# A hybrid mLSTM and attention layer on one core: cache places, weight splits and head squares moved between two attention stages

## What is computed

```
def diff_weights(scores, lam):
    p = jax.nn.softmax(scores, axis=-1)
    return p[:, :, 0] - lam * p[:, :, 1]

# prompt: blocks of 128 queries against the keys up to their chunk
s = jnp.einsum('bqhcd,bkhcd->bhcqk', qb, k) * scale      # two scores per head (c)
o = jnp.einsum('bhqk,bkhd->bqhd', diff_weights(s, lam), vf)
# sample: 16 queries of each of 8 batches against 256 cached and 16 new keys
k_all = jnp.concatenate([cache_k, dk], axis=1)
v_all = jnp.concatenate([cache_v, dv], axis=1)
# both: a norm of each head (mean of squares over 128), gains, then the projection
y_m = mlstm_readout(hm, o_gate, g)        # rms_norm(h, g) * o_gate
y_d = diff_readout(o, g, lam_init)        # rms_norm(o, g) * (1 - lam_init)
out = jnp.concatenate([y_m, y_d], axis=-1) @ w_out
```

## Time and profile before

| what | value |
|---|---|
| median of three runs | 1366.63 us (1360.15 to 1367.04) |
| the profiled execution | 1368.47 us, its span 1366.7 us |
| PE busy | 1296.9 us, 95% |
| DVE, ACT, POOL busy | 59%, 43%, 24% |
| granted clock of PE, mean | 0.966 of full |

### The profile page before, as it was taken

One profiled execution on the slowest core, in us unless ns is written; L12 is line 12 of the kernel. 1 busy time (PEld: TensorE's weight loads), 2 busy tenths in 40 slices (PEclk: granted clock), 3 DMA queues, 4 the chain that ended last, 5 costly groups with the idle time before them and its releaser, 6 DMA issues.

```text
span 1366.7 us, 23094 instructions
## 1 busy us (share of the span) xinstructions
PE 1296.9 (95%) x8072; PEld 1139.9 (83%) x8072; DVE 800.7 (59%) x1420; ACT 583.7 (43%) x1146; POOL 322.1 (24%) x276
## 2 busy tenths in 40 slices
PE   4999999999999997999999788979999999999997
PEld 3899999999878886888877455868999999988886
DVE  3767667767433755252427854258676667654484
ACT  5533434434333645422213565337344444433463
POOL 0633434343100000001010604007444443410000
PEclk9999999999999998999998698989999999999999
DMA  9655454454555741322230235131322232134563
GB/s 316 188 154 153 153 153 153 144 160 127 199 201 180 237 158 38 123 87 68 91 108 13 74 105 175 31 108 47 108 77 87 82 92 80 43 123 153 196 220 138
DMA packets 167152, 175.84 MB, mean 129 GB/s; under 512 B 10377, under 2 KB 139921, under 8 KB 167098
## 3 DMA queue, kind: packets, MB, share of 16 engines
q1 hardware_dynamic: 165754, 171.31, 39.0%
q0 software_dynamic: 1344, 3.81, 0.9%
HBM read 165.79 MB, written 9.05 MB: 128 GB/s over the span
## 4 chain that ended last, share of the span: by engine, by line
PE 90%; ACT 4%; DVE 3%; issue 2%; DMA 1%; SPq 0%; DVEq 0%; ACTq 0%
PE ps L1243 86%; DMA resid<-in_x_sample 1%; PE ps L1285 1%; PE ps L1818 1%; DVE y L2136 0%; ACT x_norm L769 0%; ACT modulated_pairs L820 0%; PE ps L1511 0%; ACT w_sums_hi L833 0%; PE ps L1564 0%; ACT h_sums_hi L843 0%; DMA k_cache<-in_cache_k 0%; PE ps L1778 0%; DVE w_lo L1934 0%; PE ps L1905 0%
## 5 line engine op out<-in xcount | busy, mean ns | idle before, releaser
L1243 PE MATMUL ps<-h_sums_hi,w_sums_hi 128*128 128x320 f32 x1216 | 376.3, 314 | 3.0 <-ACT h_sums_hi L799 2.0
L1243 PE MATMUL ps<-h_sums_hi,w_sums_lo 128*128 128x320 f32 x1216 | 371.0, 309 | 0.0
L1243 PE MATMUL ps<-h_sums_lo,w_sums_hi 128*128 128x320 f32 x1216 | 370.9, 309 | 0.0
L1934 DVE TENSOR_TENSOR w_lo<-w_raw,w_hi 128x1024 fp32r<-128x1024 f32 (+2 forms) x106 | 147.2, 1389 | 201.2 <-ACT w_hi L920 125.8
L1243 PEld LDWEIGHTS ps<-h_sums_hi,w_sums_hi 128*128 128x128 f32 x1216 | 227.4, 188 | 14.1 <-issue 10.0
L1243 PEld LDWEIGHTS ps<-h_sums_hi,w_sums_lo 128*128 128x128 f32 x1216 | 227.5, 188 | 0.0
L1243 PEld LDWEIGHTS ps<-h_sums_lo,w_sums_hi 128*128 128x128 f32 x1216 | 227.5, 188 | 0.0
L861 ACT ACTIVATE silu_gate<-silu_gate 128x320 f32<-128x320 f32 x80 | 37.9, 474 | 283.8 <-DVE silu_gate L2038 283.8
L920 ACT ACTIVATE w_hi<-w_raw 128x1024 fp32r<-128x1024 f32 x88 | 93.3, 1061 | 139.1 <-PE ps L1243 111.5
L1934 DVE TENSOR_TENSOR w_sums_lo<-w_raw,w_sums_hi 128x512 fp32r<-128x512 f32 x132 | 113.7, 865 | 44.0 <-ACT w_sums_hi L857 43.6
L1243 PE MATMUL ps<-w_hi,h_t_hi 128*128 128x512 f32 (+2 forms) x360 | 135.5, 376 | 2.8 <-DVE h_t_lo L1934 1.7
(11 more groups left out here) (333 smaller groups left out, 1832.3 us busy)
## 6 DMA issues: line engine op xcount, KB each, us to landing
w_raw<-in_w_ffn_out SPq DMA_DIRECT2D x88, 512.0 KB, 4.1
w_raw<-in_w_ffn_in SPq DMA_DIRECT2D x86, 512.0 KB, 3.8
w_raw<-in_w_ada SPq DMA_DIRECT2D x28, 1024.0 KB, 5.0
w_raw<-in_w_in SPq DMA_DIRECT2D x10, 1024.0 KB, 5.1
w_raw_start<-in_w_ada SPq DMA_DIRECT2D x8, 1024.0 KB, 8.4
w_raw<-in_w_out SPq DMA_DIRECT2D x4, 1024.0 KB, 6.4
k_cache<-in_cache_k SPq DMA_DIRECT2D x8, 512.0 KB, 5.0
v_cache<-in_cache_v SPq DMA_DIRECT2D x8, 512.0 KB, 4.1
```

Of the source, the lines that this page charges most:

```text
L1243: return pe.matmul(out, lhsT, rhs, start=start, stop=stop)
L1934: return dve.tensor_tensor(dst, raw, hi.bitcast(F32), ALU.subtract)
```

## The change

The cache has three places; batch b uses place b % 3, and nothing of it lies in `w_raw` any longer. The sync queue does not wait for group 7's splits before the caches; it waits for `st_out`, fills places 0 and 1, waits for `m_hn` and fills place 2. Then the keys of batch b wait for the transposes of batch b - 3, and the values for the output of batch b - 3, with one key load ahead of the values of the batch before. The wait for group 7's splits now stands in front of the second half of the output weights. DVE's two splits of group 7 move from steps 4 and 6 of the prompt attention to the ends of batches 2 and 4 of the sample's. The five sets of mLSTM head squares move from steps 0 to 4 to steps 6 to 10. The diff, without the lines that only replace an index by b % 3:

```diff
-        CACHE = (0, 1, 2, 3, 0, 1, 2, 0)
-
-        def cache_sems(b):
-            s = CACHE[b]
-            return (kc_landed[s], vc_landed[s]) if s < 3 else (e_landed[0], e_landed[1])
...
                 elif g == 8:
                     mixer_loads()
-                    for s in range(2):
-                        sp.wait_ge(g_hi[s], g)
-                        sp.wait_ge(g_lo[s], g)
                     continue
...
             sp.wait_ge(st_out, 16 * 11)
-            sp.wait_ge(m_hn, 2 * NT)
-            for b in range(4):
+            for b in range(3):
+                if b == 2:
+                    sp.wait_ge(m_hn, 2 * NT)
                 keys_load(b)
                 values_load(b)
-            for b in range(4, DB):
-                used = (0, 1, 2, 4)[b - 4]
-                sp.wait_ge(s_ktr, 2 * (used + 1))
-                keys_load(b)
-                sp.wait_ge(s_o, used + 1)
-                values_load(b)
-
-            sp.wait_ge(s_ktr, 2 * 4)
-            sp.wait_ge(s_o, 4)
+            for b in range(3, DB + 1):
+                if b < DB:
+                    sp.wait_ge(s_ktr, 2 * (b - 2))
+                    keys_load(b)
+                if 3 < b <= DB:
+                    sp.wait_ge(s_o, b - 3)
+                    values_load(b - 1)
+
             for s in range(2):
+                sp.wait_ge(g_hi[s], 8)
+                sp.wait_ge(g_lo[s], 8)
                 sp.dma_start(grp_view(RAW, s, 512), w_o[:, 4 * s:4 * s + 4, 512:1024]).then_inc(g_landed[s], 16)
...
-                if n < NT:
+                if 6 <= n < 6 + NT:
                     act.wait_ge(m_head, 2 * NT)
-                    head_squares(0, n, HHM[:, n, :])
+                    head_squares(0, n - 6, HHM[:, n - 6, :])
...
                 p_combine(n)
-                if n in (4, 6):
-                    grp_lo(7, (n - 4) // 2)
...
                 if b == 1:
                     dve.wait_ge(gate_bc, 2)
                     gate(1)
+                elif b in (2, 4):
+                    grp_lo(7, b // 2 - 1)
```

More of the change, by code:

```diff
@@ L243, in build @@
         C3 = 108 * KB + 264 * NT * 4 + 10 * KB
-        KC = [at("k_cache0", A0, [P, 2, 512]), at("k_cache1", A0 + 4 * KB, [P, 2, 512]), at("k_cache2", C3, [P, 2, 512]),
-              at("k_cache3", 60 * KB, [P, 2, 512])]; A0 += 8 * KB
-        VC = [at("v_cache0", A0, [P, 2, 512]), at("v_cache1", A0 + 4 * KB, [P, 2, 512]), at("v_cache2", C3 + 4 * KB, [P, 2, 512]),
-              at("v_cache3", 64 * KB, [P, 2, 512])]; A0 += 8 * KB
+        KC = [at("k_cache0", A0, [P, 2, 512]), at("k_cache1", A0 + 4 * KB, [P, 2, 512]), at("k_cache2", C3, [P, 2, 512])]; A0 += 8 * KB
+        VC = [at("v_cache0", A0, [P, 2, 512]), at("v_cache1", A0 + 4 * KB, [P, 2, 512]), at("v_cache2", C3 + 4 * KB, [P, 2, 512])]; A0 += 8 * KB
         KCT = [at("k_cache_t0", A0, [P, HD, PAST]), at("k_cache_t1", 20 * KB, [P, HD, PAST])]; A0 += 4 * KB
         QBD = at("q_blocks", A0, [P, DB, HD, 32]); A0 += 4 * KB
-        VN = [at("v_new0", A0, [DS, 512]), at("v_new1", A0 + 2 * KB, [DS, 512]), at("v_new2", 110 * KB, [DS, 512]), at("v_new3", 68 * KB, [DS, 512])]; A0 += 4 * KB
+        VN = [at("v_new0", A0, [DS, 512]), at("v_new1", A0 + 2 * KB, [DS, 512]), at("v_new2", 110 * KB, [DS, 512])]; A0 += 4 * KB
         assert A0 <= 60 * KB
@@ L525, in grp_view @@
             return T[:, s, 0:4 * n].rearrange("p (k n) -> p k n", k=4)
-        CACHE = (0, 1, 2, 3, 0, 1, 2, 0)
-        def cache_sems(b):
-            s = CACHE[b]
-            return (kc_landed[s], vc_landed[s]) if s < 3 else (e_landed[0], e_landed[1])
-        def cache_landed(b, values):
-            n = 16 * ADA_FIRST if CACHE[b] == 3 else 0
-            return cache_sems(b)[values], n + (32 if values else 16) * CACHE[:b + 1].count(CACHE[b])
         def sample_heads(T, k):
@@ L708, in _ @@
                         sp.dma_start(v, w[:, 4 * s:4 * s + 4, c0:c0 + n]).then_inc(g_landed[s], 16)
+            sp.wait_ge(st_out, 16 * 11)
             def keys_load(b):
[L711 removed]
+                sp.dma_start(KC[b % 3][:, :, :], k_cache[:, b, :, :]).then_inc(kc_landed[b % 3], 16)
             def values_load(b):
[L714 to L719 removed]
+                sp.dma_start(VC[b % 3][:, :, :], v_cache[:, b, :, :]).then_inc(vc_landed[b % 3], 16)
+                sp.dma_start(VN[b % 3][:, :], DVT[b * DS:(b + 1) * DS, NTP, :]).then_inc(vc_landed[b % 3], 16)
+            for b in range(3):
+                if b == 2:
+                    sp.wait_ge(m_hn, 2 * NT)
                 keys_load(b)
                 values_load(b)
[L722 to L730 removed]
+            for b in range(3, DB + 1):
[5 more added lines that the diff above has]
+                    values_load(b - 1)
             for s in range(2):
+                sp.wait_ge(g_hi[s], 8)
+                sp.wait_ge(g_lo[s], 8)
                 sp.dma_start(grp_view(RAW, s, 512), w_o[:, 4 * s:4 * s + 4, 512:1024]).then_inc(g_landed[s], 16)
@@ L1810, in s_key_transposes @@
             def s_key_transposes(b):
-                pe.wait_ge(*cache_landed(b, 0))
+                pe.wait_ge(kc_landed[b % 3], 16 * (b // 3 + 1))
                 if b >= 2:
@@ L1817, in s_key_transposes @@
                     for h in range(HD):
-                        q = pe.transpose(PS[:, 6 * (b % 2) + k, h * P:(h + 1) * P], KC[CACHE[b]][:, k, h * P:(h + 1) * P], ident)
+                        q = pe.transpose(PS[:, 6 * (b % 2) + k, h * P:(h + 1) * P], KC[b % 3][:, k, h * P:(h + 1) * P], ident)
                     q.then_inc(s_ktr, 1)
@@ L1844, in s_out @@
                 pe.wait_ge(s_pt, 2 * (b + 1))
-                pe.wait_ge(*cache_landed(b, 1))
+                pe.wait_ge(vc_landed[b % 3], 32 * (b // 3 + 1))
                 if b:
@@ L1851, in s_out @@
                         probs = PTS[:, k, rows] if k < 2 else PTS[0:DS, k, rows]
-                        values = VC[CACHE[b]][:, k, cols] if k < 2 else VN[CACHE[b]][:, cols]
+                        values = VC[b % 3][:, k, cols] if k < 2 else VN[b % 3][:, cols]
                         q = mm(PS[rows, 5, 0:DV], probs, values, k == 0, k == 2)
```

4 lines of the change are left out of this document (removed).

## The result

The changed kernel took 1357.77 us (median of 5 executions, 1356.97 to 1361.75) beside 1366.63 of the kernel before in the same comparison, 1360.15 to 1368.93: a ratio of 0.9947, 95% interval 0.9923 to 0.9971. With 12 further executions its mean is 1359.3 +- 1.2 us; that of the kernel before, from 102 executions beside the experiments, is 1365.5 +- 0.5. All +- in this text are 1.96 standard errors. For a true 95% they are a tenth too narrow with 12 executions and a third too narrow with five or six. So the change brings **6.2 us +- 1.3**; the forecast was 0.9 us slower, at best 5.1 faster than the median. Each execution comes with its mean granted clock of TensorE (PE): 0.9746 in the mean after, 0.9694 before. That turns out to be most of the difference.

The account below looks back on a forecast made before the run. TensorE was taken as the bound, nine tenths of the chain, so only its waits and clock matter: -2.8 prompt attention, +2.0 splits, +1.7 clock, +0.9 us in sum, 1367.5 against the median of 1366.63; range 1361.5 to 1371.5.

Parts of the forecast that it names:

- Early steps of the prompt attention: Before step 8's scores, PE waits removed with the early squares and first split: 1.5 us gained, start at 774.4.
- Steps 8 to 12: Later prompt attention: ACT's queue sets the pace, scores issued in step 12 at 791.6, 2.8 us earlier including the early steps.
- the squares as the sole bound: Steps 6 to 10: with late squares ACT needs 2.8 us a step against PE's 2.25, so ACT sets the pace.
- Loads: Cache loads in both attentions: filling places early is worth nothing, later key loads cost nothing, at worst 0.2 us.
- Splits in the sample's attention: Two splits behind batches 2 and 4 delay exponentials and PE's scores: 2.0 us lost, ends 0.5 and 6.7.
- The prediction's dearer case: Sample's attention: both splits take 3.36 us where POOL is busy throughout, making the sum 1.3 us worse.
- The clock: Sample's attention: new PE pauses of 1.7 and 2.7 us cause one clock fall, 1.7 us lost; ends none and 3.4.
- the clock that holds: Rival, sample's attention: no pause is long enough to cost the clock; -0.8 us, 1365.8; chance 0.22.
- full clock early in the prompt attention: Rival: PE back at 2.4 GHz before 774, gain 4.8, one split covered, no fall; -3.8 us, 1362.8; chance 0.16.
- squares hidden: Rival, prompt attention: ACT has room for the squares, PE goes at its own 2.25 us a step; about 1359.6; chance 0.06.
- The signs: Timeline marks in both attentions: among those for right, step 12's scores near 791.6 and half clock between 824 and 838.

Follow-up runs that it names:

- cache places alone: Kernel before with only the three cache places and the sync queue's new order; squares and splits as before: 1363.95 us, ratio 0.9981.
- early squares without splits: Changed kernel with the five sets of head squares back in steps 0 to 4; splits and caches stay changed: 1359.72 us, ratio 0.9961.
- both splits tiny: Kernel before with both output-weight splits, in steps 4 and 6 of the prompt attention, cut to 16 of 2048 columns: 1359.35 us, ratio 0.9974.
- a quarter of the squares: Changed kernel with one of four heads' squares in each of steps 6 to 10, a constant for the rest: 1358.07 us, ratio 0.9951.
- the splits back: Changed kernel with the two splits back in steps 4 and 6 of the prompt attention; squares and caches stay changed: 1364.22 us, ratio 0.9996.
- tiny splits in the prompt attention: Kernel before with splits there cut to 16 of 2048 columns: both, 1359.35 us; the second alone, 1363.39 us.
- The fillers: Changed kernel with thrown-away matmuls where PE waits anyway: 1357.52 and 1355.88 us in two runs; with 15 more ending the sample's attention, 1355.35 us.
- tiny splits there: Changed kernel with its two splits, in the sample's attention, cut to 16 of 2048 columns: 1360.81 us, ratio 0.9970.
- the squares alone: Kernel before with only the mLSTM head squares moved to steps 6 to 10; splits and cache places as before: 1362.91 us, ratio 0.9990.

## Why the prediction was wrong

It was wrong in the sign of the sum (+0.9 against -6.2), in two terms and by one thing that it left out. Without its clock term the sum is -0.8, and at equal clock the change measures -1.3 +- 0.6: the waits came out near enough in sum, if not one by one. The step that failed is the clock: +1.7 forecast, some -4.9 measured (0.0053 more mean clock at 9.3 us for 0.01).

**Early steps of the prompt attention** (-1.5): right in kind, too small. Where the splits alone differ (cache places alone, and early squares without splits), the stretch from the first scores to step 8's is 19.9 and 19.2 us: 0.7 for the first split, forecast about 0.5. Late squares take it from 19.2 to 17.4, so they free 1.8, forecast about 1.0; I had said that PE's work at half clock nearly fills these steps, but it left 0.34 and 0.67 to 0.81 us in front of two scores. Together 2.5. The other 1.2 of the pair's 3.7 lies between before and the cache places alone, which have the same work here; their clock differs. The granted clock of 760 to 778 was 0.50 before, 0.62 with the cache places alone and 0.72 in the changed kernel.

**Steps 8 to 12** (-1.3): nearly right. From the start of step 8's scores to step 12's I had 17.2 us (791.6 less 774.4); measured are 16.6 (786.15 less 769.53), after 18.5 before. The sum over ACT's queue held, and the waits of 1.05, 0.67 and 1.58 us for ACT show its pace; ahead of the longest ACT also copies the four outputs of a tile. "More than half of what they free goes to the squares" came true as well: the second split's leaving frees 4.6 us, and 2.5 are paid back by the late squares (16.6 against 14.1). What failed is the squares as the sole bound: three quarters of them away freed 1.0, not 2.8.

**Loads** (0): nothing at equal clock, 0.1 +- 0.6. PE's waits for keys were one of 0.42 us, within the sign I gave. In the mean 2.3 +- 2.0 stay unexplained; they go with a clock 0.0023 higher, and I can't say that the cache places cause it.

**Splits in the sample's attention** (+2.0): wrong; they cost 0.2 to 0.3 where batch 5's exponential stands, and nothing in the time. Two inputs failed. I let the second split start at 829.5, where the trace of before has DVE free for it at 828.35, the start of the maximum that would follow it; from there it ends under ACT's two table loads (to 830.83), which were what batch 5's exponential waited for: its row has no wait. I had charged DVE's length to an engine that was busy with its own. And I took 2.7 and 2.7 us for the splits, but they took 2.28. The Trainium skill, GPSIMD Engine Reference, section Specifications, says that POOL's way into SBUF is shared with DVE instructions that have two SBUF inputs. The prediction's dearer case by it, 3.36 us for each split, did not come; here it was POOL that paid. Its product beside the first split took 1.98 us:

```profile
815.25 1.98 POOL L2680 TENSOR_TENSOR diff_heads<-diff_heads,g_diff_rows 128x512 f32<-128x512 f32 x1 [2.29 <-ACT squares L1124]
...
819.64 1.27 POOL L2680 TENSOR_TENSOR diff_heads<-diff_heads,g_diff_rows 128x512 f32<-128x512 f32 x1 [2.41 <-ACT squares L1124]
```

So the trace agrees with the page that the two share something, and not that the split is the one to lose. The kernel before with both splits tiny shows when it does; DVE's rows (the first tiny split, a combination, the second tiny split), then POOL's:

```profile
768.37 0.17 DVE L1934 TENSOR_TENSOR w_lo<-w_raw,w_hi 128x16 fp32r<-128x16 f32 x1
...
772.75 1.37 DVE L2490 SCALAR_TENSOR_TENSOR probs<-probs,max_den 128x256 f32<-128x256 f32 x1
774.04 1.24 DVE L1934 TENSOR_TENSOR w_lo<-w_raw,w_hi 128x16 fp32r<-128x16 f32 x1
```

```profile
772.57 6.53 POOL L2692 TENSOR_TENSOR mlstm_heads<-mlstm_heads,o_gate 128x512 f32<-128x512 f32 x5
```

Sixteen columns took 1.24 us beside POOL, and 0.17 alone: 1.07 more. The whole split took 3.36 beside POOL and 2.28 alone: 1.08 more. The same surplus for 16 and for 2048 columns is not a rate that is shared. It looks as if the split first waited for the product that POOL was in the middle of (1.26 us each), and the reverse where the split had begun first; that is read from the rows, not tested. DVE's combination (1.37 us, and 1.10 the next time, in place of 0.48) is longer beside POOL too, so POOL's five products in a row were a part of what the second split seemed to cost: with both splits tiny PE still stands 1.93 us once in these steps.

**The clock** (+1.7): wrong in sign, and the largest error. I forecast one new fall from pauses of 1.7 and 2.7 us. In this profile they came as 0.71 and 0.87:

```profile
817.60 0.66 PE L1230 MATMUL ps<-k_cache_t,q_blocks 128*32 128x256 f32 x8 [0.71 <-ACT k_cache_t L1152]
...
826.02 0.66 PE L1230 MATMUL ps<-k_cache_t,q_blocks 128*32 128x256 f32 x8 [0.87 <-ACT k_cache_t L1152]
```

and 824 to 838 stayed at 2.4 GHz (not so in every profile of such a kernel: 0.85 with a quarter of the squares). The size of a fall was right: 5.4 us at half clock for 1.7 is 0.31 us for one; 0.01 of mean clock over 1360 us is 27 us at half clock, and at 9.3 us that is 0.34. The Trainium skill, TensorE: Matmul & The Clock Gate, section Terms, puts the penalty at half of the throttled time; these executions give a third. That part of it lies under waits would explain it, and is not tested. What I had left out is the credit: the pause of 2.55 us removed can take a fall of the clock with it (not always, as the kernel with the splits back shows), and I entered that only as a part of "freed" time in steps 8 to 12, not through the rest of the program. The mean clock rose by 0.0053, 4.9 of the 6.2 us. Within that the pair's fall at 744 to 750, ahead of the change, warns that one profile doesn't tell which falls the change removed; the means do.

**The rivals.** The likest to what happened are two of mine together, the clock that holds (1365.8) and full clock early in the prompt attention (1362.8), which shared nearly four tenths of the chance. Even the second stopped at 1362.8, since no term of it was a gain of clock outside its own steps. Nearest in number is "squares hidden" (1359.6, chance 0.06), but by luck: ACT had no room, and PE waited for it. **The signs**: no split between 770 and 781, the splits behind batches 2 and 4, and ACT's pace (the scores of steps 8 to 11 are 2.65, 2.82 and 2.55 us apart) came true. The scores issued in step 12 came at 786.15 and not near 791.6, 2.7 us of it from the clock ahead of the change. Batch 5's exponential came 25.8 us behind the first key transposes (824.91 less 799.12), where the sign said 25.2, but by luck: with the same splits and full clock from 799 (early squares) it comes at 22.2, and without whole splits there and at full clock at 21.8 to 21.9 (either kernel with tiny splits in the prompt attention). The splits make 0.3 of it, the half clock from 799 the other 3.6. The prompt attention was shorter by 5.7 us (46.98 against 52.70), which I had put down as a sign of being wrong, and no window at half clock lay between 824 and 838. **The range** took its bounds from prices of parts in one execution; the clock's own scatter, 15 us between executions of the same kernel, was not in it, nor a gain through the clock.

Open stays whether the higher clock of the changed kernel comes from that one pause alone. The fillers show that pauses bear on the clock here. But the pause of 2.11 us with the splits back kept full clock in its profile, and the profiles show a second place, at the end of the sample's attention, where before has 1.60 us:

```profile
833.47 0.65 PE L1230 MATMUL ps<-v_cache,probs_s_t 128*32 128x128 f32 x16 [1.25 <-ACT probs_s_t L1159]
```

All seven profiles of kernels with the splits, whole or tiny, in the prompt attention have a pause of 1.57 to 1.60 us there, and the clock is at half behind each. Of the seven with the whole splits in the sample's attention and no fillers at its end, all have 1.25 or 1.26 us, and the clock holds behind three (the changed kernel twice, and with early squares). With tiny splits there the pause is 1.37 and the clock falls. So the splits' new place may carry a part of the gain in clock. The mean of the kernel with tiny splits there, 1.7 us slower, points the same way, but at the edge of the noise.

## What to carry to other kernels

Before a wait is priced, ask what the clock does behind it: here moving two splits, of which the second made PE stand for 2.55 us, brought 5 us in the mean, 2 of it at equal clock and 3 with the clock. Price moved work by whether the next instruction in the trace has a wait for that engine: one without a wait is bound by its own engine, and there is some room in front of it. A split of 2.28 us made one such exponential 0.2 us later and another 1.4. Compare kernels by mean time and mean clock over many executions, and fill PE's unavoidable pauses with idle matmuls in front of the wait: it brought 5 us here.

## What the runs showed of the hardware

- The time of a program that is nine tenths PE follows its mean granted clock along a straight line, 9.3 us per 0.01 (255 executions, residual 1.06 us), and between executions of one program the clock ran from 0.961 to 0.977.
- Half-clock stretches differ from execution to execution on the same instructions: 744 to 750 at 0.54 in the profile of before, 1.00 with the cache places alone and 0.51 with the squares alone.
- A long pause doesn't always cost the clock: behind one of 2.11 us the granted clock was 1.00 (splits back, 776 to 784), and with one of 2.78 us it was 0.63 over the same 8 us (cache places alone).
- Throw-away matmuls in pauses keep the clock up: 0.91 without and 1.00 with them over the same 120 us of the changed kernel (0.79 in the kernel before), and 0.9746 and 0.9832 in the mean of all executions.
- Beside POOL's products a DVE split that started during one took 1.07 to 1.08 us more, whatever its size; one that had started first kept its 2.28 us, and POOL's product took 1.98 in place of 1.27.
